# The rest of every fourth weight piece in the down groups: by a subtraction on VectorE, or by an adding transfer onto a negated copy

## The reference

```python
ug = jnp.take(u, ex, axis=0)            # chosen experts' input rows
act = jax.nn.gelu(jnp.einsum('thkd,td->thk', ug, hx)) * wx
vg = jnp.take(vt, ex, axis=0)
return jnp.einsum('thk,thkd->td', act, vg)
```

## Time and profile before

| what | value |
|---|---|
| median of 3 runs | 3407.71 us (3404.61 to 3408.12) |
| profiled execution, span (no other time of it is given) | 3407.6 us |
| TensorE busy | 3368.6 us, 99% |
| VectorE busy | 2274.0 us, 67% |
| ScalarE busy | 1409.9 us, 41% |
| GpSimd busy | 634.2 us, 19% |
| mean granted TensorE clock | 0.997 of full speed |
| down groups | about 2509 to 3034 us |

### The profile page before, as it was taken

One profiled execution on the slowest core, in us unless ns is written; L12 is line 12 of the kernel. 1 busy time (PEld: TensorE's weight loads), 2 busy tenths in 40 slices (PEclk: granted clock), 3 DMA queues, 4 the chain that ended last, 5 costly groups with the idle time before them and its releaser, 6 DMA issues.

```text
span 3407.6 us, 42319 instructions
## 1 busy us (share of the span) xinstructions
PE 3368.6 (99%) x15582; PEld 2797.0 (82%) x15582; DVE 2274.0 (67%) x2275; ACT 1409.9 (41%) x1125; POOL 634.2 (19%) x342
## 2 busy tenths in 40 slices
PE   9999999999999999999999999999999999999998
PEld 7888888888888888888888888888888888888886
DVE  7664545788888888856676493555557776765556
ACT  6333343343333333343554334444443333333333
POOL 0000003300000000100000188777730000000000
PEclk9999999999999999999999999999999999999999
DMA  7555556788888888744454456767776666656552
GB/s 273 189 189 186 188 197 237 307 309 308 319 325 301 307 316 326 265 173 173 161 202 181 167 215 218 247 238 245 243 270 234 231 221 240 234 200 222 201 205 99
DMA packets 151463, 797.53 MB, mean 234 GB/s; under 512 B 15284, under 2 KB 48356, under 8 KB 64192
## 3 DMA queue, kind: packets, MB, share of 16 engines
q1 hardware_dynamic: 85168, 610.47, 48.9%
q0 software_dynamic: 27216, 149.96, 11.9%
q10 hardware_dynamic: 38976, 35.66, 3.3%
HBM read 756.09 MB, written 39.91 MB: 234 GB/s over the span
## 4 chain that ended last, share of the span: by engine, by line
PE 92%; DVE 4%; DMA 1%; ACT 1%; issue 1%; POOL 0%; ACTq 0%; DVEq 0%; SPq 0%; POOLq 0%
PE ps L1961 29%; PE ps L1963 29%; PE ps L1962 29%; PE ps L1993 2%; PE ps L2480 1%; ACT hi L576 1%; DMA adaraw<-in_w_ada 1%; DVE lo L1094 1%; DVE adaacc L1391 1%; PE ps L2110 0%; PE ps L2087 0%; DMA w_scratch<-wst 0%; PE ps L2098 0%; PE ps L2420 0%; DMA wc<-w_scratch 0%
## 5 line engine op out<-in xcount | busy, mean ns | idle before, releaser
L576 ACT CAST hi<-raw 128x2048 fp32r<-128x2048 f32 x576 | 1100.1, 1911 | 1759.0 <-PE ps L1963 1739.0
L1094 DVE TENSOR_TENSOR lo<-raw,hi 128x2048 fp32r<-128x2048 f32 x468 | 1070.9, 2291 | 630.8 <-ACT hi L576 618.2
L1961 PE MATMUL ps<-hi,hTh 128*128 128x512 f32 x3040 | 1197.0, 394 | 1.7 <-DVE hTl L1162 1.1
L1962 PE MATMUL ps<-lo,hTh 128*128 128x512 f32 x3040 | 1184.4, 390 | 0.0
L1963 PE MATMUL ps<-hi,hTl 128*128 128x512 f32 x3040 | 1184.1, 389 | 0.0
L1963 PEld LDWEIGHTS ps<-hi,hTl 128*128 128x128 f32 x3040 | 570.8, 188 | 120.4
L1961 PEld LDWEIGHTS ps<-hi,hTh 128*128 128x128 f32 x3040 | 571.4, 188 | 117.4 <-DVE hTl L1162 1.4
L1962 PEld LDWEIGHTS ps<-lo,hTh 128*128 128x128 f32 x3040 | 571.6, 188 | 113.0
L414 POOL TENSOR_TENSOR lo<-raw,hi 128x2048 fp32r<-128x2048 f32 x108 | 500.3, 4635 | 226.3 <-ACT hi L576 226.3
L1961 PE MATMUL ps<-hi,pactTh 128*128 128x512 f32 x992 | 388.2, 391 | 0.0
L1963 PE MATMUL ps<-hi,pactTl 128*128 128x512 f32 x992 | 386.3, 389 | 0.0
(11 more groups left out here) (382 smaller groups left out, 2414.2 us busy)
## 6 DMA issues: line engine op xcount, KB each, us to landing
raw<-in_w_peer SPq DMA_DIRECT2D x256, 1024.0 KB, 4.9
raw<-in_w_ffn SPq DMA_DIRECT2D x132, 1024.0 KB, 6.4
adaraw<-in_w_ada POOLq DMA_DIRECT2D x96, 1024.0 KB, 6.5
raw<-in_w_first SPq DMA_DIRECT2D x88, 1024.0 KB, 4.8
raw<-in_w_second SPq DMA_DIRECT2D x72, 1024.0 KB, 4.8
raw<-in_w_merge SPq DMA_DIRECT2D x28, 1024.0 KB, 6.6
w_scratch<-wst ACTq DMA_DIRECT2D x64, 256.0 KB, 5.4
wc<-w_scratch POOLq DMA_DIRECT2D x32, 512.0 KB, 5.2
```

Of the source, the lines that this page charges most:

```text
L576: nc.scalar.copy(hi[:, s, :], raw[:, s, :]).then_inc(hi_done, 1)
L1094: V.tensor_tensor(lo[:, s, :], raw[:, s, :], hi[:, s, :].bitcast(F32), ALU.subtract).then_inc(lo_done, 1)
L1961: T.matmul(out, th[stat], hi[:, s, cut], start=start, stop=False)
L1962: T.matmul(out, th[stat], lo[:, s, cut], start=False, stop=False)
```

## The change

In down groups 0 to 21 (`turn_rest`), ScalarE, having rounded piece 3 of the next quad, also writes its negated rounded value into `lo[3]`. GpSimd, whose loop is now written out in Python, waits for this and issues a transfer from `raw[3]` to `lo[3]` with an adding operation, both in SBUF. VectorE leaves out its subtraction for that piece. Before the first sum of down groups 1 to 21, and once before the group after them, it waits for the transfer and for the three earlier rests, and counts `lo_done` up itself (`transferred_rest`). Two semaphores are used further, `gate_st` from 12 transfers on and `gated` from 12 on. The transfer is issued behind the `load_group` of its own step, and so ahead of that of the next.

```diff
@@ GpSimd
-            with pool.Fori(1, (EARLY - 1) // 2) as m:
+            for m in range(1, (EARLY - 1) // 2):
                 for u in range(2):
                     pool.wait_ge(sem("peer_product"), 2 * m + (u - 1))
                     load_group(2 * m + u, u)
+                    pool.wait_ge(sem("gated"), 2 * m + (u - 1) + 12)
+                    pool.dma_start(lo[:, 3, :].bitcast(F32), raw[:, 3, :], accum_op=ALU.add).then_inc(sem("gate_st"), 16)
@@ ScalarE
-            def down_group(b, u, turn=True):
+            def down_group(b, u, turn=True, turn_rest=True):
 
                 for j in range(4):
                     if j == 2 and turn:
                         act.wait_ge(piece_used, 4 * b + 4 * (Q_PEER + EARLY))
                         peer_hi(b + 1, 1 - u)
                     round_piece(b + (Q_PEER + EARLY + 1), j)
+                    if j == 3 and turn_rest:
+                        nc.scalar.activation(lo[:, 3, :], raw[:, 3, :], ACT.Copy, scale=-1.0).then_inc(sem("gated"), 1)
 
             with act.Fori(0, (EARLY - 1) // 2 - 1) as m:
                 for u in range(2):
                     down_group(2 * m + u, u)
-            down_group(EARLY - 3, 0)
-            down_group(EARLY - 2, 1, turn=False)
+            down_group(EARLY - 3, 0, turn_rest=False)
+            down_group(EARLY - 2, 1, turn=False, turn_rest=False)
@@ VectorE
+            def transferred_rest(b):
+                dve.wait_ge(sem("gate_st"), 16 * b + 16 * 12)
+                dve.wait_ge(lo_done, 4 * b + (4 * (Q_PEER + EARLY) + 3))
+                dve.sem_inc(lo_done, 1)
+
             def down_group(b, u, m):
                 for j in range(4):
+                    if j == 0 and (u == 1 or not isinstance(m, int)):
+                        transferred_rest(b)
                     peer_down(b, j, 4 * b + (4 * (Q_PEER + EARLY) + j + 1))
                     if j == 2:
                         peer_lo(b + 1, 1 - u)
-                    rest_piece(b + (Q_PEER + EARLY + 1), j)
+                    if j < 3:
+                        rest_piece(b + (Q_PEER + EARLY + 1), j)
                     if j == 2:
                         early_mul(b + 2, u, m + 1)
 
-            with dve.Fori(0, (EARLY - 1) // 2 - 1) as m:
+            for u in range(2):
+                down_group(u, u, 0)
+            with dve.Fori(1, (EARLY - 1) // 2 - 1) as m:
                 for u in range(2):
                     down_group(2 * m + u, u, m)
+            transferred_rest(EARLY - 3)
```

More of the change, by code:

```diff
@@ L120 @@
     "att_o": "DVE: outputs out of PSUM", "cmb_d": "DVE: groups' maxima compared", "cmb_e": "ACT: their exponentials",
-    "o_ready": "DVE: dilated groups joined", "gate_st": "DMA: gate chunks in DRAM",
+    "o_ready": "DVE: dilated groups joined", "gate_st": "DMA: gate chunks in DRAM, then weight pieces added to their negated leading parts",
     "gl_in0": "DMA: gate in ring slot 0", "gl_in1": "slot 1", "gl_in2": "slot 2", "gl_in3": "slot 3",
-    "gated": "DVE: branch chunks gated", "merge": "DVE: chunks merged", "wo_out": "DVE: chunks of w_o added to x",
+    "gated": "DVE: branch chunks gated, then ACT: pieces rounded and negated in the rest's place", "merge": "DVE: chunks merged", "wo_out": "DVE: chunks of w_o added to x",
     "cs_done": "ACT: silu of c", "ada_in0": "DMA: even pieces", "ada_in1": "DMA: odd pieces",
```

## The result

The changed kernel takes 3490.98 us (median of 4 runs, 3488.43 to 3492.74) against 3407.91 us for the kernel before: 83 us more, ratio 1.0244 with a 95% interval of 1.0229 to 1.0258. The profiled run took 3492.3 us with a span of 3490.7 us.

What follows compares the result with a forecast made beforehand. TensorE was taken to bound the kernel. VectorE's saving counted 0; a transfer of 8.0 us against 5.65 us costs 2.35 us a group, times 22 = 51.7 us: 3407.7 + 51.7 = 3459 us, range 3404 to 3587 us.

Steps and rivals of the forecast that it cites:

- What bounds the kernel, and what VectorE's time is worth: Down groups: TensorE, busy 418.00 of 418.00 us, bounds; removing 50 us of VectorE subtractions is worth 0.
- The place: Down groups: TensorE would wait before piece 2 for VectorE's sum of piece 0, now behind the transfer; slack about 4.7 us.
- Steps 1 to 3: Down group: ScalarE casts slot 3 and negates by T + 3.83; GpSimd issues the transfer 0.30 us later, T + 4.13.
- T: Start of a down group, when ScalarE's cast of slot 3 begins; 2650.82 us in the earlier profile, period 22.69 us.
- Step 4: Down group: the adding transfer of 1 MB within SBUF, reading two operands; taken as 8.0 us.
- the length D: Adding transfer's time from issue to landing: taken as 8.0 us; each microsecond above 5.65 us stops TensorE one per group.
- Steps 5 and 6: After landing: VectorE wakes and passes its waits, 0.29 us; sum of piece 0, 1.22 us; TensorE starts 0.11 us later.
- rival D: Clock falls in stalls: one piece at 1.2 GHz per group, 120 us on top of mechanism A, 3579 us; chance 0.04.
- the clock is under 1.00: Down groups: a granted TensorE clock below 1.00 was one listed sign that the prediction is wrong.
- mechanism A: Down groups: an adding transfer of 6 to 10 us stops TensorE before piece 2; 3415 to 3503 us; chance 0.50.
- Raw slot 3, the moved loads, the order of VectorE's work: Down groups: slot 3's reload and moved loads stay hidden, loads with 3.8 us to spare; only sum 0 is critical.

Runs made afterwards that it cites:

- wait behind the sum: Changed kernel, but VectorE takes piece 0 out of its banks before it waits for the transfer; 3408.2 us against 3408.25 us for the kernel before.
- both remedies: Changed kernel, but ScalarE negates before it rounds and GpSimd holds the next loads until the transfer lands; 3411.31 us against 3410.13 us for the kernel before.
- loads held: Changed kernel, but GpSimd waits for the transfer's landing before issuing the next loads of weights and hidden values; 3439.81 us, ratio 1.0086 to the kernel before.
- negation first: Changed kernel, but ScalarE writes the negated part before the leading part, so the transfer starts earlier; 3426.34 us, ratio 1.0054 to the kernel before.
- 1536 columns: Changed kernel, but the transfer adds only the first 1536 of 2048 columns; 3442.68 us, ratio 1.0096 to the kernel before.
- every second group: Changed kernel, but the transfer serves only odd down groups, 11 times instead of 22; 3445.4 us, ratio 1.0101 to the kernel before.

## Why the prediction was right, and where it was short

**What bounds the kernel, and what VectorE's time is worth.** Right. 50 us less of VectorE's subtractions bought nothing. Where the stop is removed (wait behind the sum, both remedies) the time is that of the kernel before within 0.1%.

**The place.** Right: TensorE stops before piece 2, for the sum of piece 0, which stands behind the wait. The first experiment moves that sum alone, and the loss is gone.

**Steps 1 to 3.** ScalarE's negation took 1.91 us and hid. The issue came at T + 4.03 (forecast T + 4.13), 0.30 us behind ScalarE as forecast. That it is so short because the code is written out is not shown: in the same written-out loop the load of `wc` at 2510.47 us came 0.56 us behind the VectorE product that released it (2508.68 + 1.23 = 2509.91 us).

**Step 4, the length D.** 8.1 us was measured and 8.0 forecast, but this was partly luck. With the loads held back the transfer takes 7.0 us, close to the 7.3 us composed from two reads. The other 1.1 us comes from the loads issued right behind it. I had treated those loads as moved and hidden, and asked only whether they would be late themselves. They were not late; they made the transfer before them late. The 2 MB row from which I took 8.0 us had the right size for another reason.

The Trainium skill's rule in "Collectives: The Full Stack" ("The bandwidth ceiling: the fold count and why AG ≠ RS ≠ AR"), that the second source read makes a reducing transfer long, fits what was measured in direction: 8.1 us against 5.1 us for a copy in the same place. That page of the Trainium skill gives its model for ring collectives of three or more ranks and not for a transfer inside SBUF. The estimate of 6.2 us worked out from it is 0.8 us under the 7.0 us that the transfer takes with the loads held. The runs don't show whether the read or the adder sets the rate.

**Steps 5 and 6.** From the median landing to the sum 2657.28 - (2648.76 + 8.1) = 0.42 us (forecast 0.29); from the sum's end, 2658.50 us, to the product 0.14 us. With these the stop is 2.5 us a group instead of 2.35, and 22 x 2.5 = 55 us, against the forecast 51.7.

**The term that was missing** is the clock. I had it as rival D, at 0.04, and set it aside because in the earlier trace rows TensorE lost 2.0 us and stayed at 1.00. That was one stop in one trace, before the transposes of the first down group, and some such stops do leave the clock up. Eight of the traces have that stop, with 1.6 to 2.2 us of idle time, and in two of them (negation first, 2.23 us, and loads held, 2.19 us) the clock fell behind it. The stretch of the earlier trace rows with the negation first, where 1.00 stood before:

```profile
2506.00:2528.00 22.00, 20.91 (x94) 17.36 (x95) 12.57 (x8) 8.45 (x7) 1.29 (x2) 0.92 0.58 211
```

So the row that spoke against rival D was a chance outcome. The measured price is 1.6 us behind 16 of 22 stops, 26 us, and filling the stops gave back the same 26 us. 55 + 26 = 81 us, against 83 measured. The prediction had named "the clock is under 1.00" as a sign that it is wrong. That sign came: 0.96 in the stretch of the earlier trace rows, so its mechanism A was right but not the whole. My price for the rival was 5.45 us a group, over three times too high, since only eight products or so run slowly and not a whole piece. Behind the shorter stops, 0.8 us (negation first) and 1.3 us (1536 columns, loads held), the clock never fell.

**Raw slot 3, the moved loads, the order of VectorE's work.** Right as far as the traces show: no further wait appears.

So the total came out 32 us above the middle of the forecast and inside its range; it lies inside rival A's 3415 to 3503 us too. But by A alone 3491 us would have needed D = 9.4 us (5.65 + 83 / 22), and D was 8.1. 26 us of this are the missing term and 3 us the longer stop; 2 to 3 us are not accounted for.

## What to carry to other kernels

A wait put into an engine's queue delays everything behind it there, so look first for what frees a buffer of the bounding engine: moving one sum ahead of the wait turned 83 us of loss into none. When you put a transfer on a path, look also at what is issued right *behind* it on the same queue. And work given to idle engines gains nothing while TensorE is busy all the time.

## What the hardware showed that I had not expected

- Stops of TensorE before piece 2 with 2.1 to 2.6 us of idle time in the profile (2.4 to 2.8 us of lost time) lowered its clock to half for some 3.4 us in 16 of 22 cases, in 6 of 11 with every second group, and in the one such case with the loads held. Stops that cost 1.3 us and less never did in these traces. What decides whether a longer stop lowers the clock is not shown. Filling the stop with useless products made the kernel 26 us faster.
- Two loads of 512 KB, issued 0.55 and 1.3 us behind an adding transfer of 1 MB on the same queue, lengthened it from 7.0 to 8.1 us.
- Within SBUF an adding transfer of 1 MB took 8.1 us where a copy took 5.1 us, both with the loads behind them.
